# Inverting the delta-rule matrices of a hybrid mixer: levels 1 to 5 as two 64x64 blocks per head on tiles of the TensorE array

## The reference

```python
lower = jnp.where(strict, jnp.einsum('bhnid,bhnjd->bhnij', kb, k) * gamma, 0.0)
tmat = lower + jnp.eye(C, dtype=lower.dtype)
solve = lambda rhs: lax.linalg.triangular_solve(tmat, rhs, left_side=True, lower=True,
                                                unit_diagonal=True)
u = solve(v * beta[..., None])
w = solve(kb * jnp.exp(g)[..., None])
```

## Time and profile before

| | |
|---|---|
| median of 3 runs | 1997.1 us (1996.66 to 1997.33) |
| span of the profiled execution | 1993.6 us |
| what lies around the span (1997.1 - 1993.6) | 3.5 us |
| TensorE busy / VectorE busy | 1966.2 us (99%) / 1289.4 us (65%) |
| first inversion (from the first coupling product to the last level) | 605.2 to 646.7 us |
| second inversion | 667.9 to 710.0 us |

### The profile page before, as it was taken

One profiled execution on the slowest core, in us unless ns is written; L12 is line 12 of the kernel. 1 busy time (PEld: TensorE's weight loads), 2 busy tenths in 40 slices (PEclk: granted clock), 3 DMA queues, 4 the chain that ended last, 5 costly groups with the idle time before them and its releaser, 6 DMA issues.

```text
span 1993.6 us, 27062 instructions
## 1 busy us (share of the span) xinstructions
PE 1966.2 (99%) x10127; PEld 1665.0 (84%) x10127; DVE 1289.4 (65%) x1816; ACT 747.9 (38%) x979; POOL 110.2 (6%) x166
## 2 busy tenths in 40 slices
PE   9999999999999999999999999999999999999998
PEld 7888888887789989888888888888887888888887
DVE  7877577875748876877678853363346542567676
ACT  5321222344565434322222333212235432635553
POOL 1010000000003300100001000000000000000000
PEclk9999999999999999999999999999999999999999
DMA  9555455622110003655555532343234422144543
GB/s 357 176 195 179 167 195 171 203 96 85 64 53 21 1 22 106 211 184 179 176 191 165 181 127 84 104 163 114 82 108 148 169 85 105 43 175 153 190 173 123
DMA packets 51450, 275.30 MB, mean 138 GB/s; under 512 B 6081, under 2 KB 6401, under 8 KB 31649
## 3 DMA queue, kind: packets, MB, share of 16 engines
q1 hardware_dynamic: 31536, 203.71, 29.2%
q0 software_dynamic: 19104, 69.41, 10.8%
q10 hardware_dynamic: 720, 0.95, 0.1%
HBM read 272.99 MB, written 1.05 MB: 137 GB/s over the span
## 4 chain that ended last, share of the span: by engine, by line
PE 90%; DVE 5%; ACT 3%; issue 1%; DMA 1%; SPq 0%; DVEq 0%; ACTq 0%
PE ps L1187 15%; PE ps L1189 15%; PE ps L1188 15%; PE ps L1424 6%; PE ps L1426 6%; PE ps L1425 6%; PE ps L1199 6%; PE ps L1200 3%; PE ps L2737 2%; PE ps L2738 2%; PE ps L2739 2%; DVE w_lo L775 1%; ACT w_hi L507 1%; PE ps L2246 1%; PE ps L2258 1%
## 5 line engine op out<-in xcount | busy, mean ns | idle before, releaser
L1187 PE MATMUL ps<-h_parts,w_lo 128*128 128x512 f32 (+1 forms) x1424 | 538.1, 378 | 3.5 <-DVE w_lo L775 2.2
L1189 PE MATMUL ps<-h_parts,w_hi 128*128 128x512 f32 (+1 forms) x1424 | 534.0, 375 | 0.0
L1188 PE MATMUL ps<-h_parts,w_hi 128*128 128x512 f32 (+1 forms) x1424 | 533.7, 375 | 0.0
L775 DVE TENSOR_TENSOR w_lo<-w_raw,w_hi 128x2048 fp32r<-128x2048 f32 (+3 forms) x189 | 392.4, 2076 | 184.6 <-ACT w_hi L507 184.5
L507 ACT ACTIVATE w_hi<-w_raw 128x2048 fp32r<-128x2048 f32 (+3 forms) x191 | 332.0, 1738 | 417.1 <-PE ps L1426 254.0
L783 DVE SCALAR_TENSOR_TENSOR ada_product<-ada_w,silu_c 128x1024 bf16<-128x1024 f32 x256 | 313.1, 1223 | 22.3 <-DVE ada_product L783 10.5
L1187 PEld LDWEIGHTS ps<-h_parts,w_lo 128*128 128x128 f32 x1424 | 268.1, 188 | 53.2 <-DVE w_lo L775 3.5
L1189 PEld LDWEIGHTS ps<-h_parts,w_hi 128*128 128x128 f32 x1424 | 268.0, 188 | 48.8
L1188 PEld LDWEIGHTS ps<-h_parts,w_hi 128*128 128x128 f32 x1424 | 268.2, 188 | 46.8
L519 ACT ACTIVATE sil<-ps 128x512 f32<-128x512 f32 x66 | 39.5, 598 | 481.3 <-PE ps L1189 481.3
L1424 PE MATMUL ps<-hid_parts,w_lo 128*128 128x512 f32 x468 | 182.1, 389 | 0.0
(11 more groups left out here) (368 smaller groups left out, 2569.7 us busy)
## 6 DMA issues: line engine op xcount, KB each, us to landing
w_raw<-in_w_up SPq DMA_DIRECT2D x88, 1024.0 KB, 4.8
ada_w<-in_ada POOLq DMA_DIRECT2D x128, 512.0 KB, 3.9
w_raw<-in_w_down SPq DMA_DIRECT2D x24, 768.0 KB, 4.3
w_raw<-in_w_ret_t SPq DMA_DIRECT2D x16, 1024.0 KB, 4.9
w_raw<-in_w_down SPq DMA_DIRECT2D x24, 640.0 KB, 3.9
w_raw<-in_w_ab SPq DMA_DIRECT2D x14, 1024.0 KB, 4.8
w_raw<-in_w_down SPq DMA_DIRECT2D x9, 1024.0 KB, 4.9
ada<-in_ada SPq DMA_DIRECT2D x8, 1024.0 KB, 22.2
```

Of the source, the lines that this page charges most:

```text
L775: dve.tensor_tensor(w_lo[parts_of(s, slot)][:, 0:elems], raw_of(s, slot)[:, 0:elems], w_hi[parts_of(s, slot)][:, 0:elems].bitcast(F32), AL ...
L1187: pe.matmul(out, lo, rhs_hi(k), start=first and k == 0, stop=False)
L1188: pe.matmul(out, hi, rhs_lo(k), start=False, stop=False)
L1189: mm = pe.matmul(out, hi, rhs_hi(k), start=False, stop=last and k == nk - 1)
```

## The change

Levels 1 to 5 never couple the first 64 rows of a chunk with the last 64. The change keeps, of each 128x128 matrix, only the two diagonal 64x64 blocks in these levels: rows 0 to 63 hold the first block and rows 64 to 127 the second, side by side with nothing between, so that a buffer of 4 heads is 128x256 instead of 128x512. Each matmul of a group becomes two, on the tile of the TensorE array at rows and columns 0 to 63 and on the one at 64 to 127; both write the same PSUM bank, on different partitions. `diag` holds the diagonal blocks of the coupling; `coup` keeps the whole and is multiplied later (`off_diagonal`). The transpose of level 0 becomes an ordinary product with the identity. Level 6 crosses the halves: `cross_blocks` and `correct_blocks` read the off-diagonal blocks of `coup` and the two block inverses. The whole transpose `inv_t` is put together at level 5 by VectorE and GpSimd (which also clears it once), and level 6 writes its off-diagonal blocks.

```diff
--- before.py
+++ after.py
-    decay, coup, cut, xb, nrm, trn, turned, k_decay, eg, q_eg = ([None, None] for _ in range(10))
+    decay, coup, diag, cut, xb, nrm, trn, half_t, turned, k_decay, eg, q_eg = ([None, None] for _ in range(12))
...
-        nrm[c], _ = put(f"inv{c}", [P, 2, DNH, P], at=s0[2])
+        nrm[c], _ = put(f"inv{c}", [P, 2, DNH, W], at=s0[2])
         k_decay[c], _ = put(f"k_decay{c}", [P, 2, DNH, P], at=s0[2])
         trn[c], _ = put(f"inv_t{c}", [P, 2, DNH, P], at=s0[4])
         coup[c], _ = put(f"coup{c}", [P, DNH, P], at=s0[6])
-        cut[c], _ = put(f"cut{c}", [P, DNH, P], at=s0[7])
-        xb[c], _ = put(f"xbuf{c}", [P, DNH, P], at=s0[8])
-        turned[c], _ = put(f"turned{c}", [P, DNH, P], at=s0[9])
+        cut[c], _ = put(f"cut{c}", [P, DNH, W], at=s0[7])
+        diag[c], _ = put(f"diag{c}", [P, DNH, W], at=s0[7] + KB)
+        xb[c], _ = put(f"xbuf{c}", [P, DNH, W], at=s0[8])
+        turned[c], _ = put(f"turned{c}", [P, DNH, W], at=s0[8] + KB)
+        half_t[c], _ = put(f"half_t{c}", [P, 2, DNH, W], at=s0[9])
         eg[c], _ = put(f"grown{c}", [P, 2, DNH, P], at=at_ring + (0, 16)[c] * KB + 4 * KB)
...
     def pool_deltanet(pool):
 
+        for c in range(2):
+            inv(pool, iv_dve, INV_DVE, c, 0, "ARG")
+            pool.memset(trn[c][:], 0.0)
         for s in range(2):
-            for l in range(1, LEVELS):
+            for l in range(1, LEVELS - 1):
                 for c in range(2):
                     if l < 3:
                         inv(pool, iv_dve, INV_DVE, c, s, ("SYS", "T0")[l - 1])
                     else:
                         inv(pool, iv_pe, INV_PE, c, s, f"X{l - 1}")
-                    pool.tensor_tensor((xb if l == 1 else cut)[c][:], coup[c][:], over(levels[:, l * P:(l + 1) * P], 4), ALU.mult) \
+                    if s == 1 and l == 1 and c == 0:
+                        inv(pool, iv_pool, INV_POOL, 1, 0, "HALF")
+                    pool.tensor_tensor((xb if l == 1 else cut)[c][:], diag[c][:], over(levels[:, l * W:(l + 1) * W], 4), ALU.mult) \
                         .then_inc(iv_pool[c], 1)
+            for c in range(2):
+                inv(pool, iv_dve, INV_DVE, c, s, "T4")
+                if c == 0:
+                    inv(pool, iv_pool, INV_POOL, 1, s, f"M{LEVELS - 2}")
+                for q in range(2):
+                    op = pool.tensor_copy(crossed_full(trn[c], q, other=True),
+                                          crossed(half_t[c][BLOCKS[q]], LEVELS - 2, other=True))
+                op.then_inc(iv_pool[c], 1)
...
             for h in range(DNH):
-                mm = pe.matmul(bank(0, c)[:, h * P:(h + 1) * P], (xb if l == 1 else cut)[c][:, h, :],
-                               crossed(nrm[c], l, h), start=True, stop=True)
+                for blk in BLOCKS:
+                    mm = pe.matmul(halves(0, c)[blk, h * W:(h + 1) * W], (xb if l == 1 else cut)[c][blk, h, :],
+                                   crossed(nrm[c][blk], l, h), start=True, stop=True)
             mm.then_inc(iv_pe[c], 1)
 
         def correct(c, l):
             inv(pe, iv_act, INV_ACT, c, s, f"X{l}")
-            if l < LEVELS - 1:
-                for h in range(DNH):
-                    mm = pe.matmul(bank(1, c)[:, h * P:(h + 1) * P], turned[c][:, h, :], xb[c][:, h, :],
+            for h in range(DNH):
+                for blk in BLOCKS:
+                    mm = pe.matmul(halves(1, c)[blk, h * W:(h + 1) * W], turned[c][blk, h, :], xb[c][blk, h, :],
                                    start=True, stop=True)
-                mm.then_inc(iv_pe[c], 1)
+            mm.then_inc(iv_pe[c], 1)
+            if l == 1:
+                inv(pe, iv_dve, INV_DVE, c, s, "OFF")
             for h in range(DNH):
-                mm = pe.matmul(bank(2, c)[:, h * P:(h + 1) * P], xb[c][:, h, :], turned[c][:, h, :],
-                               start=True, stop=True)
+                for blk in BLOCKS:
+                    mm = pe.matmul(halves(2, c)[blk, h * W:(h + 1) * W], xb[c][blk, h, :], turned[c][blk, h, :],
+                                   start=True, stop=True)
+            mm.then_inc(iv_pe[c], 1)
+
+        def cross_blocks(c):
+            inv(pe, iv_dve, INV_DVE, c, s, f"N{LEVELS - 2}")
+            for h in range(DNH):
+                for q in range(2):
+                    mm = pe.matmul(halves(0, c)[BLOCKS[1 - q], h * W:(h + 1) * W], coup[c][BLOCKS[q], h, BLOCKS[1 - q]],
+                                   nrm[c][BLOCKS[q], q, h, :], start=True, stop=True)
+            mm.then_inc(iv_pe[c], 1)
+
+        def correct_blocks(c):
+            inv(pe, iv_act, INV_ACT, c, s, f"X{LEVELS - 1}")
+            inv(pe, iv_dve, INV_DVE, c, s, f"T{LEVELS - 2}")
+            inv(pe, iv_pool, INV_POOL, c, s, "HALF")
+            for h in range(DNH):
+                for q in range(2):
+                    mm = pe.matmul(halves(2, c)[BLOCKS[q], h * W:(h + 1) * W], xb[c][BLOCKS[1 - q], h, :],
+                                   trn[c][BLOCKS[1 - q], 1 - q, h, BLOCKS[1 - q]], start=True, stop=True)
             mm.then_inc(iv_pe[c], 1)
...
-        for l in range(2, LEVELS):
+        for l in range(2, LEVELS - 1):
             cross(0, l)
             correct(1, l - 1)
             correct(0, l)
             cross(1, l)
+        cross_blocks(0)
+        correct(1, LEVELS - 2)
+        correct_blocks(0)
+        cross_blocks(1)
         if s == 1:
             pe_scan_keys(pe, s, 0, 0)
         else:
             pe_scan_values(pe, s, 0, 0)
-        correct(1, LEVELS - 1)
+        correct_blocks(1)
...
-            dve.tensor_tensor(coup[c][:], coup[c][:], bank4(2, c), ALU.mult).then_inc(iv_dve[c], 1)
+            for blk in BLOCKS:
+                op = dve.tensor_tensor(diag[c][blk], coup[c][blk, :, blk], bank4(2, c)[blk, :, blk], ALU.mult)
+            op.then_inc(iv_dve[c], 1)
             inv(dve, iv_dve, INV_DVE, c, s, "SYS")
-            dve.tensor_tensor(cut[c][:], coup[c][:], over(levels[:, 0:P], 4), ALU.mult).then_inc(iv_dve[c], 1)
+            dve.tensor_tensor(cut[c][:], diag[c][:], over(levels[:, 0:W], 4), ALU.mult).then_inc(iv_dve[c], 1)
...
+
+        def off_diagonal(c):
+            dve.tensor_tensor(coup[c][:], coup[c][:], bank4(2, c), ALU.mult).then_inc(iv_dve[c], 1)
 
         joined(0)
         coupled(0)
@@ -2454,7 +2522,9 @@
         joined(1)
         begun(0)
         coupled(1)
+        off_diagonal(0)
         begun(1)
+        off_diagonal(1)
...
+                if l < LEVELS - 2:
+                    part = crossed(half_t[c][:], l)
+                    op = dve.tensor_tensor(part, part, parted(halves(2, c), l), ALU.subtract)
+                else:
+                    for q, blk in enumerate(BLOCKS):
+                        op = dve.tensor_tensor(crossed_full(trn[c], q), crossed(half_t[c][blk], l),
+                                               parted(halves(2, c)[blk], l), ALU.subtract)
+                op.then_inc(iv_dve[c], 1)
...
-            part = crossed(trn[c], LEVELS - 1)
-            dve.tensor_tensor(part, part, parted(bank(2, c), LEVELS - 1), ALU.subtract).then_inc(iv_dve[c], 1)
+            for q, blk in enumerate(BLOCKS):
+                op = dve.tensor_scalar(trn[c][blk, 1 - q, :, BLOCKS[1 - q]],
+                                       halves(2, c)[blk].rearrange("p (h d) -> p h d", h=DNH), -1.0, None, ALU.mult)
+            op.then_inc(iv_dve[c], 1)
```

More of the change, by code:

```diff
@@ L66, in constants @@
     const = np.concatenate([np.asarray(b, f32) for b in blocks] + [np.cos(ang), (signed * np.sin(ang)).astype(f32)], axis=1)
-    levels = np.zeros((LEVELS, P, P), f32)
-    for s in range(LEVELS):
+    levels = np.zeros((LEVELS, P, W), f32)
+    jw, nw = i[:, None] % W, np.arange(W)[None, :]
+    for s in range(LEVELS - 1):
         b = 1 << s
-        m = ((n // (2 * b)) == (j // (2 * b))) & ((n // b) % 2 == 1) & ((j // b) % 2 == 0)
-        levels[s] = m | m.T
-    levels = np.ascontiguousarray(levels.transpose(1, 0, 2).reshape(P, LEVELS * P))
+        below = ((nw // (2 * b)) == (jw // (2 * b))) & ((nw // b) % 2 == 1) & ((jw // b) % 2 == 0)
+        above = ((nw // (2 * b)) == (jw // (2 * b))) & ((nw // b) % 2 == 0) & ((jw // b) % 2 == 1)
+        levels[s] = below | above
+    levels[LEVELS - 1] = nw == jw
+    levels = np.ascontiguousarray(levels.transpose(1, 0, 2).reshape(P, LEVELS * W))
     ahead = (np.arange(3 * P)[None, :] - P - np.arange(P)[:, None]).astype(f32)
@@ L201, in build @@
         resid[d], _ = put(f"resid{d}", [P, DNH, P], at=at_ring + 8 * KB + (4 + 2 * d) * KB)
-    levels, _ = put("levels", [P, LEVELS * P], at=at_ring + 28 * KB)
+    levels, _ = put("levels", [P, LEVELS * W], at=at_ring + 28 * KB)
     g_rest, g_exps = (small[:, n:n + 64].rearrange("p (w n) -> p w n", w=2) for n in (160, 224))
@@ L2164, in bank4, with halves @@
         return bank(n, d).rearrange("p (h d) -> p h d", h=4)
+    def halves(n, d):
+        return bank(n, d)[:, 0:DNH * W]
     def both(ap):
@@ L2237, in turn @@
```

(4 more changed lines are left out.)

56 lines of the change are left out of this document (34 added, 22 removed).

## The result

The changed kernel takes **1978.7 us** (median of 4 runs, 1977.74 to 1979.37); the kernel before takes 1996.88 us on the same chip (4 runs, 1996.61 to 1997.33). The ratio is 0.9909, with a 95% interval of 0.9897 to 0.9921. The prediction was 1982 us. The profiled execution took 1979.37 us with a span of 1977.7.

A forecast was written before the change was run, and what follows sets the result against it. TensorE, busy for 99% of the span, bounds the kernel, with VectorE close under it. Inversions give -8.1 and -8.0 us, changes of shape +1, net -15: span 1978.6, plus 3.5 around it, 1982 us; range 1977 to 2000.

The forecast's parts named there:

- group of 16: TensorE's tile groups in the levels: two tiles run at once, so 16 records take 0.47 us where eight took 0.89.
- ahead of level 1: From the first coupling product to level 1: VectorE sets the pace, with halved operations and shorter transpose waits, -1.5 us each inversion.
- levels 1 to 4: VectorE sets levels 1 to 3, TensorE and the copy's way level 4: 16.2 us, -5.0 us in each inversion.
- levels 5 and 6: End of each inversion, set by VectorE's chain: 8.2 and 8.1 us, so -1.6 in the first and -1.5 in the second.
- changes of shape: TensorE switching between whole-array products and tiles, about eight times an inversion, some 0.1 us each: +1 us for both.
- third rival: Records have a floor: if TensorE starts one every 70 ns at soonest, a group takes 1.12 us; 2009 us, chance 0.16.
- the tiles don't overlap: The first rival, on TensorE's groups: a group stays at 0.89 us, only -2 us for both inversions, 1995 us; chance 0.14.
- what GpSimd takes away: VectorE's delay beside GpSimd's masks at levels 2 and 3: half of 0.94 us, 0.5, giving 4.6 us a level.
- fourth rival: VectorE is held by GpSimd or signals up to 0.5 us more in each of ten levels, 1987 us; 0.52 with the forecast.
- second rival: TensorE's clock falls to 0.50 in the levels: 1990 us with half of them in it, 1998 with all; chance 0.18.
- the prediction's own sign: In the first inversion, the forecast is wrong if the clock reads 0.50 between 612 and 640 us.
- Nothing behind it uses the time up: Behind the inversions, scan and output-weight products keep their order, so the span falls by the whole 15 us to 1978.6.

The follow-up runs named there:

- e1: The changed kernel with each group's 16 records issued block by block, eight per tile, instead of alternating between the tiles: 1983.5 us, ratio 0.9936 to the kernel before.
- e8c: The changed kernel with GpSimd making half of each mask ahead of the whole one from level 2 on: 1980.09 us, ratio 0.9920 to the kernel before.
- e3: The changed kernel with the split of the next weights moved from level 5 to the scan's second run: 1973.97 us, ratio 0.9889 to the kernel before.
- e4: The changed kernel with VectorE making each last stage before that set's k_decay, set 1's k_decay behind the scan's v_new: 1970.88 us, ratio 0.9872 to before.
- e0_after: The changed kernel run and profiled again, unchanged: 1975.21 us, ratio 0.9897 to the kernel before.
- e0_before: The kernel before, unchanged, profiled a second time: 1996.73 us (one run).
- the three moves: The changed kernel with set 1's key product at level 4, the weights' split in the scan's second run, last stages before k_decay: 1970.92 and 1970.4 us.

## Why the prediction was right, step by step

| step | predicted | measured in the first profile | |
|---|---|---|---|
| group of 16 | 0.47 us | 0.47 | |
| ahead of level 1, first / second | -1.5 / -1.5 | -1.4 / -3.0 | clock in part |
| levels 1 to 4, each inversion | -5.0 | -7.6 | VectorE |
| levels 5 and 6, first / second | -1.6 / -1.5 | +0.2 / -1.4 | clock |
| changes of shape | +1 | 0.1 us each on TensorE, not separated | |
| sum | -15 | -21.0 in the stage | |
| start-up | 0 | +3.1 | clock, other code |
| last FFN and what else is behind the stage | 0 | +2.0 | open |

**The group.** Right, and with it the answer on the first and third rival. The records are 29 ns apart on average, so neither "the tiles don't overlap" (0.89 us a group) nor a floor from 58 ns a record holds. Both tiles write one PSUM bank on different partitions. The kernel before has no such case, its attention writes two banks, so how far its 0.63 us carries over was open; the 0.47 us, and the 0.58 with the tiles out of turn in e1, say that here the two run at the same time. Single starts on different tiles follow each other after 22 ns, in e1 after 5 ns, and on one tile (the tiles inferred as in e1) after 58 ns. No run shows the floor of 70 ns or more to which the prediction gave 0.16. The third rival's 0.118 us with 32 moving columns does go with the whole stationary: at a clock of 1.00 records with a stationary of 128x128 start every 0.112 us with 1 moving column (L1458 of the first profile, 11.31 to 11.87 us) as with 128, those with one of 64x64 every 0.058 us on a tile.

**Levels 1 to 4.** The mechanism was right: VectorE without a gap sets levels 1 to 3, TensorE and the copies set level 4, and GpSimd's masks hide. The size was off, 13.55 us for 16.2. The step that failed is "what GpSimd takes away": I took half of the 0.94 us for levels 2 and 3 because the masks have half the columns. e8c shows that columns are not what counts: what counts is how much of a mask is left when VectorE starts. Before, 1.07 us of it was left (622.23 + 1.28 - 622.44, the first of the two in the earlier trace rows) and the product took 0.93 longer, at level 3 0.93 was left (627.70 + 1.27 - 628.04) and it took 0.80 longer; after, 0.05 is left and it takes nothing; in e8c 0.57 was left and it took 0.43 longer. That is 2 x 0.5 us in an inversion. The other 1.6 comes from adding up durations that overlap by 0.08 us, six in each of levels 1 to 3 (6 x 0.08 x 3 = 1.4), and from level 4 at 2.64 instead of 2.9. The fourth rival, VectorE held more than counted, had the sign wrong.

**Levels 5 and 6.** The path was right (split, `k_decay`, last stages on VectorE, the values ahead of the last products), and its length nearly: 8.2 us predicted, 8.7 measured where the clock stays at 1.00, so -1.1 for -1.6. Of the 0.5, 0.27 is the scan's first values: the chain has 1.16 us for them, as in the kernel before, and I had put 0.89. In the first profile the clock fell behind the pause that this path leaves on TensorE, and that took 1.4 us more, which leaves +0.2. That is the second rival at a place where I had not put it: I expected it in the levels, where TensorE turned out to be busy for 3.4 of 4 us at 1.00 throughout. By the prediction's own sign, a clock of 0.50 between 612 and 640 us, the first profile counts against it (0.50 from 637 us on), the two later ones for it. e3 and e4 split the path further: of VectorE's two long operations the split was worth only 0.4 us, `k_decay` 1.3.

**Ahead of level 1.** The first is right between two profiles that both have a stretch at 0.50 there (10.6 and 9.1 us from the first coupling product to level 1). That is luck in part: in e0_after, with the clock at 1.00, it is 8.2 us, -2.4. In the second the kernel before lost the clock (0.50 in the earlier trace rows, 674 to 675 us), the kernel after doesn't, in any profile, and it is 8.3 us for 11.4. No profile of the kernel before has the clock at 1.00 there, so how much of the 1.5 us more the clock is stays open, as does why it falls there and not elsewhere.

**The changes of shape.** The 0.1 us each is right on TensorE in e0_after: from the last record of a group to the first of the next it is 0.11 us between whole-array groups and 0.20 from a whole-array group to tiles; between tile groups it is 0.04 and from tiles to the whole array 0.15. Most of it lies beside VectorE's work; what the stage pays for it no run here separates.

**The sum and the time.** Too small a gain in the levels and the second start (-2.6 x 2 and -1.5) met a loss in the first tail (+1.8), the start-up (+3.1) and behind the stage (+2.0). The last is a step that failed: "Nothing behind it uses the time up". The order there is the same as forecast, but the last FFN takes 1.9 us more in every profile of the changed kernel, and the cause stays open. That the forecast came within 3.3 us of the measured time, inside its range, thus rests partly on errors against each other: for the stage alone it said 15 us and the trace has 21.0, or 23.2 where the clock stays whole after the change (and is at 0.50 twice before it). The repetitions, 1975.21 and 1976.53 us, lie just below the range's 1977. The 3.5 us that I put around the span were wrong as well: in both kernels the time is 1.6 to 1.7 us over the span of the same execution (1979.37 - 1977.7; 1996.73 - 1995.1). The first profile of before was an execution shorter than the timed ones; against e0_before it reached the stage 1.4 us earlier (602.1 and 603.5 us).

## What to carry to other kernels

When one engine gets faster, add up the next engine's operations by the distance between their starts, not by their recorded durations, and ask which of two engines that meet will now start first: a wait can go, as VectorE's for GpSimd did (2.15 us for a product before, 1.22 after). Before an item in the chain is moved, work out the second-longest way past it: the split of 1.23 us was worth 0.4, `k_decay` of 1.23 us was worth all of it, and putting the last products first paid in full only once both things that stood between the two last stages were gone. With tiles, issue the records so that neighbours lie on different tiles: a group took 0.47 us so, and 0.58 with eight records a tile in a row. And compare the code that the change doesn't touch as well: here 1.9 us of the gain were lost in it, and the variants differ by as much.

## What was not expected of the hardware

- Two 64x64 tiles on different rows and columns ran at the same time into one PSUM bank: 29 ns a record on average in the kernel after, 53 to 59 ns from slot to slot in e1.
- TensorE paired records over a distance of several in the order: with eight records a tile in a row, twelve of the sixteen still started within 0.01 us of another record (e1).
- Of GpSimd and VectorE on operands in SBUF the one that started first kept its time (a mask 0.73 us in e8c), and the other took longer by most of what the first had left: 0.57 us left cost 0.43 (e8c), 0.93 cost 0.80 and 1.07 cost 0.93 (before), and a half mask of 0.45 us took 1.35 when it started inside a product (e8c). Operations of VectorE with PSUM operands kept their 0.41 us beside a mask (621.12 us in the first profile, the mask at 621.10).
- The granted clock fell to 0.50 at the same place in some executions of one kernel and not in others, behind the same instructions (tail of the first inversion: after, not e0_after); a stretch cost 0.7 to 1.4 us.
- The same 704 records of the last FFN take 123.9 us in five of the kernels and 125.8 us in the five others, at a clock of 1.00, and repeated profiles of a kernel agree (before twice, after three times, the three moves twice). The cause is open.
